# Rests of the gated values made three blocks early in the v pass of a PEER layer

## The chip, the cores and the metric

The kernel runs on one core of a Trainium2 chip. The metric is the device time of one execution in microseconds; the time given is the median of the runs. The profile is one execution of the same program, read with the hardware profiler.

## The reference, cut to what matters

The program is a chain of four transformer layers over 256 tokens of width 1024, in float32. The first two end in a PEER layer: 8 heads choose 16 each of 16384 experts per token, and the output is a sum over the chosen experts' rows of `v`, weighted by the gelu of the hidden values times the gate.

```python
def block(args):
    xb, eb, gb = args
    h = jnp.einsum('td,thkd->thk', xb, u[eb], preferred_element_type=jnp.float32)
    a = (jax.nn.gelu(h, approximate=False) * gb).astype(xb.dtype)
    return jnp.einsum('thk,thkd->td', a, v[eb])
```

Only the last line, for each of the two PEER layers, is touched by the change.

## The kernel before, in words

The kernel does not gather experts. It computes the hidden value of every one of the 16384 experts for all 256 tokens (the u pass), multiplies it by a gate that is zero for an expert that was not chosen, and multiplies the resulting 256 x 16384 matrix by all of `v` (the v pass). Both passes go in 128 blocks of 128 experts. A block of `u` or `v` is 128 x 1024 float32, 512 KB.

TensorE works on float32r values, and a float32 product is made of three matmuls (`mm3`, line 354): each operand is split into a rounded value and its rest (value minus rounded value), and rounded x rounded, rounded x rest and rest x rounded are added up. So each operand costs one rounding on ScalarE and one subtraction on VectorE.

The v pass, block n (of `peer_pe`, lines 1328 to 1341): for two halves of the tokens and two halves of the width one `mm3` each, 12 matmuls of 512 columns. They read

- `Ar[n % 4]`: the gated values of block n, 128 x 256, rounded (`gated_act`, line 1343, on ScalarE) and their rest (`gated_dve`, line 1352, on VectorE), four buffers;
- `whi[n']`: the block of `v`, rounded (`round_block`, line 1199, on ScalarE), three buffers, taken in turn;
- `ring_rest`: the rest of that block (`rest_block`, line 1207, on VectorE). It lies over `ring`: the rest is written in place of the raw block, in one of seven slots, which SyncE's queue fills from memory (`load`, line 275) as soon as the block seven before has been used.

The names: `("y", l, n)` is signalled by TensorE (semaphore `psum_complete`) when block n of the v pass of layer l is done. `round_block` of v block k waits for `y` of block k - 3, which frees its `whi` buffer; `gated_act` of block n waits for `y` of block n - 4. Every rest, that of a gated block and that of a v block alike, counts one semaphore up, `weights_rest` (`lo`), in VectorE's order; every rounding counts up `weights_rounded` (`hi`). TensorE waits at the head of block n for `lo.at(("Ar", l, n))` and `lo.at(("v", l, n))`.

Each engine has one instruction stream, written out by hand, and takes it in order. In the v pass they are:

```python
for n in range(125):                          # ScalarE, lines 1382 to 1384
    round_block(act, l, 128 + n + 3)
    gated_act(act, l, n + 3)
for n in range(128):                          # VectorE, lines 1417 to 1420
    gated_dve(dve, l, n)
    if n < 126:
        rest_block(dve, l, 130 + n)
```

(`round_block(act, l, 128 + k)` is v block k.) So after `y` of block k ScalarE rounds v block k + 3 and then gated block k + 3; VectorE makes the rest of v block k + 3, and behind it the rest of gated block k + 2. GpSimd does nothing in the v pass.

The functions that the diff touches, with the line numbers of the profile:

Of the kernel before, what the change touches and what calls it, by code (L numbers as in the profile page):

```python
# [195 lines left out]
def build(nc, io, out, consts, where):  # L196
    ctx = ExitStack()
    with ctx:
# [90 lines left out]
        def raw(name):  # L289
            return ring[:, slot[name], :]  # L290
# [72 lines left out]
        def step(e, ins):  # L363

            sig = vec if e.name == "V" else acted if e.name == "A" else gps
            ins.then_inc(*sig.next())
            e.wait_ge(*sig.now())
# [92 lines left out]
        def project_all(e, projs, xk, ahead=0, hooks=None):  # L460

            names = [(pr["name"], g) for pr in projs for g in range(2)]
            for i in range(-1, len(names)):
                if ahead <= i + 1 < len(names):
                    if e.name == "S":
                        load_unit(e, names[i + 1])
                    elif e.name == "A":
                        round_unit(e, names[i + 1])
                    elif e.name == "V":
                        rest_unit(e, names[i + 1])  # L470
                if i < 0:
                    continue
                if e.name == "P":
                    project_pe(e, i // 2, projs[i // 2], i % 2, xk)
                elif e.name in "VA" and i % 2:
                    project_out(e, i // 2, projs[i // 2])
                for f in (hooks or {}).get(i, ()):
                    f(e)
# [714 lines left out]
        def block_name(l, k):  # L1193
            return ("u", l, k) if k < 128 else ("v", l, k - 128)

        def used(l, k):
            return ("h", l, k) if k < 128 else ("y", l, k - 128)

        def round_block(act, l, k):

            name = block_name(l, k)
            act.wait_ge(*ready[name])
            if k >= 3:
                act.wait_ge(*psum.at(used(l, k - 3)))
            act.activation(whi[:, k % 3, :], raw(name), ACT.Copy).then_inc(*hi.next(name))

        def rest_block(e, l, k):

            name = block_name(l, k)
            e.wait_ge(*hi.at(name))  # L1210
            ins = e.tensor_tensor(ring_rest[:, slot[name], :], raw(name), whi[:, k % 3, :].bitcast(F32), ALU.subtract)
            ins.then_inc(*(glo if k < BEFORE else lo).next(name))
# [34 lines left out]
        def gates_act(act, l, m):  # L1247

            act.wait_ge(*vec.at(("gated", l, m)))
            d = slice(DONE[m], 128)  # L1250
            act.activation(area[:, d, 8 * m:8 * m + 8], gates_at(2 * (m % 2))[:, d, :], ACT.Copy,
                           scale=1.0 / 32768.0).then_inc(*acted.next(("gates", l, m)))
# [9 lines left out]
        def hidden_act(act, l, n):  # L1262

            g, pv = GATED[n], ps[:, 6 + n % 2, 0:T]
            act.wait_ge(*psum.at(("h", l, n)))
            if g:
                if n >= 2 and GATED[n - 2]:
                    act.wait_ge(*vec.at(("h", l, n - 2)))
                ins = act.activation(hA[:, n % 2, 0:g], pv[:, 0:g], ACT.Gelu)
                if g < T:  # L1270
                    ins.then_inc(*acted.next())
            if g < T:
                ins = act.activation(area[:, n, g:T], pv[:, g:T], ACT.Gelu)
            ins.then_inc(*acted.next(("h", l, n)))
# [20 lines left out]
        def scores_out(e, l):  # L1295
            for k, (t, n0) in enumerate(SCORES):
                if "VA"[k % 2] != e.name:
                    continue
                e.wait_ge(*psum.at(("scores", l, t, n0)))
                o, i = Sc[:, t, n0:n0 + 4, :], bank(k).rearrange("p (n k) -> p n k", n=4)  # L1300
                if e.name == "V":
                    e.tensor_copy(o, i).then_inc(*vec.next(("scores", l, t, n0)))
                else:
                    e.activation(o, i, ACT.Copy).then_inc(*acted.next(("scores", l, t, n0)))
# [38 lines left out]
        def gated_act(act, l, n):  # L1343

            act.wait_ge(*vec.at(("gated", l, 31)))
            if GATED[n]:
                act.wait_ge(*vec.at(("h", l, n)))
            if n >= 4:
                act.wait_ge(*psum.at(("y", l, n - 4)))
            act.activation(Ar[:, n % 4, 0, :], area[:, n, :], ACT.Copy).then_inc(*hi.next(("Ar", l, n)))  # L1350

        def gated_dve(dve, l, n):
            dve.wait_ge(*hi.at(("Ar", l, n)))
            dve.tensor_tensor(Ar[:, n % 4, 1, :], area[:, n, :], Ar[:, n % 4, 0, :].bitcast(F32), ALU.subtract).then_inc(
                *lo.next(("Ar", l, n)))

        def peer_act(act, l, xk):
            project_all(act, projP[l], xk, 2)
            scores_out(act, l)
            for k in range(3):  # L1360
                round_block(act, l, k)
            wide_at = {16: ("dA", 0), 17: ("dA", 1), 18: ("tB", 0), 19: ("tB", 1)}
            for kind, n in EVENTS:
                if kind == "h":
                    round_block(act, l, n + 3)
                    hidden_act(act, l, n)
                    if n in wide_at:
                        what, t = wide_at[n]
                        d = tb[t]
                        o, i = (d["dAr"], d["dA"]) if what == "dA" else (d["tBr"], d["tf"][:, :, 1, :])  # L1370
                        act.wait_ge(*vec.at(("dA", l, t)))
                        act.activation(o, i.unsqueeze(3).to_broadcast(H16), ACT.Copy).then_inc(*acted.next(("wide", l, t, what)))
                    if n == 32:
                        for t in both:
                            act.wait_ge(*vec.at(("ex", l, t)))
                            act.activation(tb[t]["res"][:, 2, :, :], tb[t]["res"][:, 2, :, :], ACT.Exp).then_inc(
                                *acted.next(("ex", l, t)))
                elif kind == "gate":
                    gates_act(act, l, n)
            for n in range(3):  # L1380
                gated_act(act, l, n)
            for n in range(125):
                round_block(act, l, 128 + n + 3)
                gated_act(act, l, n + 3)

        def peer_pool(pool, l, xk):
            for n in range(BEFORE):
# [2 lines left out]
        def peer_dve(dve, l, xk):  # L1390
            project_all(dve, projP[l], xk, 2)
            scores_out(dve, l)
            topk_dve(dve, l)
            for t in both:
                dve.wait_ge(*psum.at(("res", l, t)))
                dve.tensor_copy(jT[:, :, t * 128:(t + 1) * 128], ps[:, 4 + t, 0:256].rearrange("p (r k) -> p r k", r=2)).then_inc(
                    *vec.next())
                dve.tensor_scalar(gr[:, t * 128:(t + 1) * 128], ps[:, 4 + t, 256:384], 32768.0, None, ALU.mult).then_inc(
                    *vec.next(("gr", l, t)))
            dve.wait_ge(*vec.now())  # L1400
            step(dve, dve.tensor_copy(gk[:, 0, :], gr))
            step(dve, dve.tensor_tensor(gr, gr, gk[:, 0, :], ALU.subtract))
            dve.tensor_copy(gk[:, 1, :], gr).then_inc(*vec.next(("gk", l)))
            one_hots_dve(dve, l, 0)
            for k in range(BEFORE, BEFORE + 2):
                rest_block(dve, l, k)
            for kind, n in EVENTS:
                if kind == "gate":
                    gates_dve(dve, l, n)
                elif kind == "h" and n >= BEFORE:  # L1410
                    rest_block(dve, l, n + 2)
                    if GATED[n - 1]:
                        hidden_dve(dve, l, n - 1)
                    if n % 2 == BEFORE % 2 and 1 <= GATED[n] // 8 < 32:
                        one_hots_dve(dve, l, GATED[n] // 8)
            hidden_dve(dve, l, 127)
            for n in range(128):
                gated_dve(dve, l, n)
                if n < 126:
                    rest_block(dve, l, 130 + n)  # L1420

        def topk_dve(dve, l):

# [141 lines left out]
        for h in range(6):  # L1565
            for t in range(2):
                n = 128 * (t + 1)
# [264 lines left out]
        for h in range(8):  # L1832
            kv = h // 4
            o = 64 * kv
            for t in range(2):
# [14 lines left out]
                n = 128 * (t + 1)  # L1850
# [4 lines left out]
        for h in range(8):  # L1855
            o = 64 * (h % 2)
            for t in range(2):
                n = 128 * (t + 1)
# [584 lines left out]
```

## Time and profile before

| | |
|---|---|
| median of 3 runs | 3196.44 us (3195.13 to 3197.36) |
| profiled execution, its own time | 3195.85 us |
| span of the profiled execution | 3194.0 us |
| TensorE matmuls busy, share of the span | 2989.4 us, 94% |
| VectorE busy | 1987.9 us, 62% |
| ScalarE busy | 1328.6 us, 42% |
| GpSimd busy | 371.0 us, 12% |
| mean granted TensorE clock | 0.935 of full speed |
| moved from and to memory | 478.74 MB, mean 150 GB/s |

The span runs from the first to the last instruction; some 2 us of the execution's own time lie around it. The v pass of the first PEER layer lies at 683 to 1056 us of the span, that of the second at 1723 to 2098 us. "PE" is TensorE's matmuls, "PEld" its weight loads, which run beside the matmuls; "DVE" is VectorE, "ACT" ScalarE, "POOL" GpSimd, "SP" SyncE, whose queue issues the transfers.

### The profile page before, as it was taken

The page shows a single profiled execution, that of the slowest core. Times are in us where ns is not written, and L with a number is a line of the kernel's source. Part 1 is how long each engine was busy: PE and PEld are TensorE (multiplying, and loading weights), DVE is VectorE, ACT ScalarE, POOL GpSimd, SP SyncE. Part 2 cuts the span into 40 slices and gives each one's busy share as a digit, 9 for nine tenths or more (in the row PEclk, how much of TensorE's full clock was granted, in tenths as well). Part 3 has the DMA queues.
Part 4 walks back from the last instruction along what each step waited for, and adds up shares of the span by engine and source line. Part 5 has one row for each costly group of instructions (what it writes and reads, how often), then busy time and mean ns, then how long its engine had stood idle before and what let it go on. Part 6 is the DMA issues. An engine that isn't in the chain of part 4 may idle for free.

```text
span 3194.0 us, 46441 instructions
## 1 busy us (share of the span) xinstructions
PE 2989.4 (94%) x19008; PEld 2639.5 (83%) x19008; DVE 1987.9 (62%) x3739; ACT 1328.6 (42%) x2130; POOL 371.0 (12%) x205
## 2 busy tenths in 40 slices
PE   8879999999999798999999999979989998989997
PEld 7779999987777787999998777767668997878997
DVE  4668978955555556796895555564665545455555
ACT  3333544444444343454444444432333433433332
POOL 0015910000000111591000000021000001010000
PEclk9889999999999998999999999987579999879999
DMA  5244544455555534454445445543025554324553
GB/s 189 90 140 139 177 148 159 153 178 180 182 178 181 159 129 133 140 178 147 158 159 171 179 181 181 178 129 119 1 87 162 175 179 160 115 54 159 177 180 112
DMA packets 223316, 478.74 MB, mean 150 GB/s; under 512 B 27120, under 2 KB 108032, under 8 KB 223104
## 3 DMA queue, kind: packets, MB, share of 16 engines
q1 hardware_dynamic: 220144, 473.29, 45.6%
q8 instruction: 150, 2.46, 0.3%
q10 hardware_dynamic: 2960, 2.49, 0.2%
q14 instruction: 62, 0.51, 0.1%
HBM read 474.14 MB, written 1.57 MB: 149 GB/s over the span
## 4 chain that ended last, share of the span: by engine, by line
PE 78%; DVE 12%; ACT 6%; POOL 2%; issue 1%; DMA 0%; ACTq 0%; DVEq 0%; SPq 0%; POOLq 0%
PE ps L133 76%; DVE ring_rest L148 4%; ACT whi L139 4%; PE ps L136 2%; POOL ring_rest L148 2%; DVE big L156 1%; DVE Ar L148 1%; DVE st L152 1%; ACT big L139 1%; DVE spl L148 1%; DVE xb L156 1%; DVE big L148 1%; DVE st L156 0%; DVE st L172 0%; DVE xr L148 0%
## 5 line engine op out<-in xcount | busy, mean ns | idle before, releaser
L139 ACT ACTIVATE whi<-ring 128x1024 fp32r<-128x1024 f32 x512 | 542.7, 1061 | 747.1 <-PE ps L133 747.0
L133 PE MATMUL ps<-xr,whi 128*128 128x256 f32 x4096 | 753.4, 286 | 11.0 <-POOL ring_rest L148 10.5
L148 DVE TENSOR_TENSOR ring_rest<-ring,whi 128x1024 fp32r<-128x1024 f32 x412 | 503.6, 1223 | 383.9 <-ACT whi L139 383.9
L133 PE MATMUL ps<-whi,Ar 128*128 128x512 f32 x2048 | 671.3, 399 | 12.6 <-DVE Ar L148 4.5
L133 PE MATMUL ps<-xr,spl 128*128 128x256 f32 (+1 forms) x5256 | 653.0, 287 | 7.9 <-DVE xr L148 4.0
L133 PEld LDWEIGHTS ps<-xr,spl 128*128 128x128 f32 (+1 forms) x5256 | 647.7, 194 | 14.2 <-issue 5.4
L133 PEld LDWEIGHTS ps<-xr,whi 128*128 128x128 f32 x4096 | 643.2, 193 | 13.8 <-DVE big L178 8.6
L148 DVE TENSOR_TENSOR spl<-ring,spl 128x1024 fp32r<-128x1024 f32 (+4 forms) x356 | 401.9, 1170 | 378.3 <-ACT spl L139 378.1
L133 PE MATMUL ps<-xr,ring_rest 128*128 128x256 f32 x2048 | 581.9, 284 | 0.0
L133 PEld LDWEIGHTS ps<-whi,Ar 128*128 128x128 f32 x2048 | 384.9, 188 | 158.5 <-DVE Ar L148 72.1
L139 ACT ACTIVATE spl<-ring 128x1024 fp32r<-128x1024 f32 (+3 forms) x384 | 366.3, 1002 | 273.7 <-PE ps L133 265.9
L133 PE MATMUL ps<-ring_rest,Ar 128*128 128x512 f32 x1024 | 401.4, 392 | 0.0
L133 PEld LDWEIGHTS ps<-xr,ring_rest 128*128 128x128 f32 x2048 | 395.8, 193 | 0.0
L139 ACT ACTIVATE big<-ps 128x256 f32<-128x256 f32 (+25 forms) x415 | 152.7, 368 | 352.1 <-PE ps L133 188.5
L148 POOL TENSOR_TENSOR ring_rest<-ring,whi 128x1024 fp32r<-128x1024 f32 x100 | 267.3, 2691 | 163.2 <-ACT whi L139 162.6
L148 POOL TENSOR_TENSOR spl<-ring,spl 128x1024 fp32r<-128x1024 f32 (+1 forms) x28 | 57.3, 2069 | 1894.7 <-ACT spl L139 1894.7
L133 PE MATMUL ps<-spl,xr 128*128 128x512 f32 (+2 forms) x1152 | 245.6, 374 | 6.9 <-DVE spl L148 3.8
L133 PEld LDWEIGHTS ps<-spl,xr 128*128 128x128 f32 x1152 | 204.6, 196 | 44.6 <-DVE spl L148 4.6
L133 PEld LDWEIGHTS ps<-ring_rest,Ar 128*128 128x128 f32 x1024 | 192.9, 188 | 32.3
L133 PE MATMUL ps<-big 128*128 128x64 f32 (+9 forms) x752 | 207.6, 423 | 4.6 <-DVE big L148 1.8
L133 PEld LDWEIGHTS ps<-big 128*128 128x128 f32 (+3 forms) x752 | 156.1, 270 | 61.4 <-issue 38.4
L133 PE MATMUL ps<-spl,Ar 128*128 128x512 f32 x768 | 183.6, 395 | 0.0
(107 smaller groups left out, 2202.0 us busy)
## 6 DMA issues: line engine op xcount, KB each, us to landing
ring<-in_peer_u_dram SPq DMA_DIRECT2D x256, 512.0 KB, 3.5
ring<-in_peer_v_dram SPq DMA_DIRECT2D x256, 512.0 KB, 3.4
ring<-in_moe_w_gate_dram SPq DMA_DIRECT2D x64, 512.0 KB, 4.1
ring<-in_moe_w_up_dram SPq DMA_DIRECT2D x64, 512.0 KB, 4.2
ring<-in_moe_w_down_dram SPq DMA_DIRECT2D x64, 512.0 KB, 4.1
ring<-in_peer_w_q_dram SPq DMA_DIRECT2D x32, 512.0 KB, 4.2
ring<-in_sb_w_in_dram SPq DMA_DIRECT2D x24, 512.0 KB, 4.3
ring<-in_ab_w_in_dram SPq DMA_DIRECT2D x20, 512.0 KB, 4.8
```

What stands on the lines that cost most here:

```text
L133: return self.e.matmul(o, l, r, start=start, stop=stop)
L136: return self.e.transpose(o, i, ident)
L139: return self.e.activation(o, i, f, **k)
L148: return self.e.tensor_tensor(o, a, b, op)
L152: return self.e.tensor_scalar(o, a, s1, None, op0)
L156: return self.e.scalar_tensor_tensor(out=o, in0=a, scalar=s, in1=b, op0=op0, op1=op1)
```

## The change

VectorE makes the rests of gated blocks 0, 1 and 2 ahead of its loop, and in the loop that of block n + 3 behind the rest of v block n + 2. ScalarE rounds gated block n + 3 ahead of v block n + 3 instead of behind it. Nothing is added or taken away: both kernels have the same instructions, apart from waits.

```diff
@@ ScalarE, peer_act
             for n in range(3):
                 gated_act(act, l, n)
             for n in range(125):
+                gated_act(act, l, n + 3)
                 round_block(act, l, 128 + n + 3)
-                gated_act(act, l, n + 3)
@@ VectorE, peer_dve
             hidden_dve(dve, l, 127)
-            for n in range(128):
+            for n in range(3):
                 gated_dve(dve, l, n)
-                if n < 126:
-                    rest_block(dve, l, 130 + n)
+            for n in range(126):
+                rest_block(dve, l, 130 + n)
+                if n + 3 < 128:
+                    gated_dve(dve, l, n + 3)
```

VectorE's stream where the v pass of the first layer begins, with the semaphores that an instruction waits for. `Ar<-big,Ar` is the rest of a gated block, `ring_rest<-ring,whi` that of a v block; `big<-hA,big` belongs to the u pass. Before (gated 0, v 2, gated 1, v 3, gated 2, v 4):

```order
L148 TENSOR_TENSOR big<-hA,big 128x256 [waits scalar_result] x2
L148 TENSOR_TENSOR Ar<-big,Ar 128x256 [waits weights_rounded]
L148 TENSOR_TENSOR ring_rest<-ring,whi 128x1024
L148 TENSOR_TENSOR Ar<-big,Ar 128x256 [waits weights_rounded]
L148 TENSOR_TENSOR ring_rest<-ring,whi 128x1024 [waits weights_rounded]
L148 TENSOR_TENSOR Ar<-big,Ar 128x256
L148 TENSOR_TENSOR ring_rest<-ring,whi 128x1024 [waits weights_rounded]
```

With the change (gated 0, 1, 2, then v 2, gated 3, v 3, gated 4, v 4):

```order
L148 TENSOR_TENSOR big<-hA,big 128x256 [waits scalar_result] x2
L148 TENSOR_TENSOR Ar<-big,Ar 128x256 [waits weights_rounded] x3
L148 TENSOR_TENSOR ring_rest<-ring,whi 128x1024
L148 TENSOR_TENSOR Ar<-big,Ar 128x256 [waits weights_rounded]
L148 TENSOR_TENSOR ring_rest<-ring,whi 128x1024 [waits weights_rounded]
L148 TENSOR_TENSOR Ar<-big,Ar 128x256 [waits weights_rounded]
L148 TENSOR_TENSOR ring_rest<-ring,whi 128x1024 [waits weights_rounded]
```

The two kinds still alternate, but each gated rest in the loop belongs to a block two later than before, and it now carries a wait for ScalarE of its own.

ScalarE's stream at the same place, `Ar<-big` being a rounded gated block and `whi<-ring` a rounded v block (v 3, v 4 and v 5 here). Before:

```order
L139 ACTIVATE hA<-ps 128x256 [waits vector_result]
L139 ACTIVATE Ar<-big 128x256 x3
L139 ACTIVATE whi<-ring 128x1024 [waits psum_complete,ring6_landed]
L139 ACTIVATE Ar<-big 128x256
L139 ACTIVATE whi<-ring 128x1024 [waits psum_complete,ring0_landed]
```

With the change:

```order
L139 ACTIVATE hA<-ps 128x256 [waits vector_result]
L139 ACTIVATE Ar<-big 128x256 x4
L139 ACTIVATE whi<-ring 128x1024 [waits psum_complete,ring6_landed]
L139 ACTIVATE Ar<-big 128x256
L139 ACTIVATE whi<-ring 128x1024 [waits psum_complete,ring0_landed]
```

Gated block 3 comes ahead of the first wait for TensorE, and from there on a rounded v block is followed by gated block k + 4 instead of k + 3 (k being the block whose end ScalarE waited for).

## Rows read from the trace of the kernel before

**Rows 1.** Page, part 4: the chain that ended last, shares of the span by engine
```profile
PE 78%; DVE 12%; ACT 6%; POOL 2%; issue 1%; DMA 0%; ACTq 0%; DVEq 0%; SPq 0%; POOLq 0%
```
**Rows 2.** Windows: us, busy (x instructions) by engine, clock, DMA share, GB/s
```profile
450.00:650.00 200.00, 199.74 (x1883) 198.02 (x1882) 173.64 (x257) 95.61 (x202) 0.00 (x0) 1.00 0.49 158
690.00:1048.00 358.00, 354.36 (x1473) 268.14 (x1472) 191.80 (x246) 166.76 (x246) 0.00 (x0) 1.00 0.54 181
1732.00:2088.00 356.00, 351.81 (x1466) 267.19 (x1465) 190.39 (x244) 166.50 (x245) 0.00 (x0) 1.00 0.52 180
```
**Rows 3.** Waits, 682 to 1058 us: waiter, releaser, us in total, times, longest
```profile
ACT whi L139 <- PE ps L133: 195.6, 125, 3.0
DVE ring_rest L148 <- ACT whi L139: 171.2, 125, 2.8
PEld ps L133 <- DVE Ar L148: 36.3, 84, 2.5
```
**Rows 4.** Chain that ended last, 896 to 902 us: start, us, what
```profile
896.01 3.04 PE ps L133 x12
...
899.13 1.07 ACT whi L139
...
900.23 1.23 DVE ring_rest L148
901.45 0.35 DVE Ar L148
...
901.84 3.04 PE ps L133 x12
```
**Rows 5.** Timeline, weight loads at four block heads [idle before <-releaser]
```profile
688.76 0.19 PEld L133 LDWEIGHTS ps<-whi,Ar 128*128 128x128 f32 x1 [0.51 <-DVE Ar L148]
...
1047.87 0.19 PEld L133 LDWEIGHTS ps<-whi,Ar 128*128 128x128 f32 x1 [0.46 <-DVE Ar L148]
...
1730.60 0.19 PEld L133 LDWEIGHTS ps<-whi,Ar 128*128 128x128 f32 x1 [0.49 <-DVE Ar L148]
...
2089.66 0.19 PEld L133 LDWEIGHTS ps<-whi,Ar 128*128 128x128 f32 x1 [0.51 <-DVE Ar L148]
```
**Rows 6.** Timeline, matmuls between two stalls, first and last: start, us
```profile
902.18 0.39 PE L133 MATMUL ps<-ring_rest,Ar 128*128 128x512 f32 x1
...
907.19 0.39 PE L133 MATMUL ps<-whi,Ar 128*128 128x512 f32 x1
```
**Rows 7.** Timeline, matmuls of the last blocks, first and last
```profile
1048.20 0.39 PE L133 MATMUL ps<-ring_rest,Ar 128*128 128x512 f32 x1
...
1055.99 0.39 PE L133 MATMUL ps<-whi,Ar 128*128 128x512 f32 x1
```
**Rows 8.** Timeline of VectorE, the rest of v block 2
```profile
682.81 1.22 DVE L148 TENSOR_TENSOR ring_rest<-ring,whi 128x1024 fp32r<-128x1024 f32 x1
```
**Rows 9.** Tile Ar: durations ns min/median/max, first and last start
```profile
L139 ACT ACTIVATE Ar<-big x256: 397/400/407, 682.0 to 2090.6; 128x256 fp32r<-128x256 f32 x128
L148 DVE TENSOR_TENSOR Ar<-big,Ar x256: 415/418/421, 682.5 to 2092.2; 128x256 fp32r<-128x256 f32 x128
```
**Rows 10.** Tile in_peer_v_dram: issues of v blocks, and time to landing
```profile
DMA to landing us min/median/max: 3.2/3.4/4.9
```
**Rows 11.** Waits of SyncE's queue, 690 to 1060 us
```profile
SPq L193 <- PE ps L133: 324.1, 126, 2.8
```
**Rows 12.** Windows across the head of the second v pass
```profile
1716.00:1724.00 8.00, 5.73 (x44) 5.43 (x43) 4.75 (x7) 4.17 (x9) 0.00 (x0) 0.95 0.57 195
1724.00:1727.00 3.00, 3.00 (x9) 2.37 (x9) 0.60 (x2) 0.00 (x0) 0.00 (x0) 0.56 0.01 5
```
**Rows 13.** Timeline, the slow matmuls at that head
```profile
1724.21 1.06 PE L133 MATMUL ps<-whi,Ar 128*128 128x512 f32 x2
1725.06 0.63 PE L133 MATMUL ps<-ring_rest,Ar 128*128 128x512 f32 x1
```

## The prediction

> **What bounds the kernel now.** I read the chain of waits first, because it says which engine has to become shorter. Three quarters of it are TensorE's [rows 1]; DVE has 12% and ACT 6%, so there are places where TensorE waits for those two. Next I put windows over the stages, since the change touches two stages only. The second thing to see is in [rows 2]: in the u pass (450 to 650 us) TensorE has no gap, 199.74 of 200 us. In the two v passes it is short by 3.6 and 4.2 us of 358 and 356, which looks like nothing. But the end of a matmul is modelled, and the 0.39 us row of a matmul whose successor comes 0.23 us later covers a part of any gap behind it. So busy time can't size a short stall; only distances between starts can. The waits show that the stall is there: the weight loads waited 84 times for the rest of a gated block in the first v pass, 36.3 us in all [rows 3]. One of these, 2.5 us, is the head of the pass. The others average (36.3 - 2.5) / 83 = 0.41 us.
>
> The chain through the middle of a v pass tells why [rows 4]. It is a closed loop. Twelve matmuls of block k (3.04 us with the drain of the last), then ACT rounds v block k + 3 (1.07), DVE makes its rest (1.23), DVE makes the rest of gated block k + 2 (0.35 beyond its overlap with the instruction ahead), and then block k + 2 may start. From one head to the other it is 901.84 - 896.01 = 5.83 us, for two blocks. What TensorE waits for is the last of these, a 128x256 subtraction of 0.42 us [rows 9] whose inputs have been there for most of a block: its rounding, done after `y` of block k - 1, is over before this loop begins. It is late only because it stands behind the rest of v block k + 3, which nobody needs until the block after. That is a matter of order, and order is what the change alters.
>
> **What a block costs without the stall.** I need the distance of two matmuls where nothing waits. Between two stalls, from the second matmul of one head to the last but none before the next, 22 distances take 907.19 - 902.18 = 5.01 us, 0.2277 us each [rows 6]. That stretch has one full turn of ACT and DVE work in it and most of a second. In the last blocks of the pass, 34 distances take 1055.99 - 1048.20 = 7.79 us, 0.2291 us each [rows 7]. I take the middle, 0.2284; a block of 12 is then 2.741 us (2.732 to 2.749). The stalled pace comes from the heads of blocks 2 and 125 [rows 5]: (1047.87 - 688.76) / 123 = 2.920 us a block in the first pass, (2089.66 - 1730.60) / 123 = 2.919 in the second.
>
> At one place a page would give another figure. The rows say 0.228 us per matmul of 512 columns at a granted clock of 1.00 [rows 2, 6]. The Trainium skill, page "TensorE: Matmul & The Clock Gate", section "Back-to-back issue gap", has a fixed 2.5 ns above columns / 2.4 for isolated gaps, 216 ns at 512 columns; by it a free block would be 2.59 us, and the gain nearly double. The measured stretches, in which no wait is recorded, do not agree, so the sum goes by them.
>
> **The change part by part.** *VectorE.* In the loop the gated rest behind v block n + 2 becomes that of block n + 3 instead of n + 1. Its input is ready in time: ACT rounds gated block n + 3 right behind v block n + 2, 0.40 us [rows 9], and is done at some 1.07 + 0.40 = 1.5 us after `y` of block n - 1, while DVE is busy with the v rest until 1.07 + 1.23 = 2.3 us after it [rows 4]. So the new wait for ACT before each gated rest costs nothing, and nothing but the next v rest is queued behind it. The gated rest is then done 2.7 us after `y` of block n - 1 and used three blocks, 8.2 us, after it, so it leaves TensorE's path. That takes out the whole stall: 2.920 - 2.741 = 0.179 us a block, times 123 blocks, 22.0 us in each v pass and 44 us in both. *What is late next.* A block's head now waits for the rest of its own v block: 3.04 + 1.07 + 1.23 us and some 0.1 us of hand-overs after the head of a block three earlier, 5.4 us, against 3 x 2.741 = 8.2 us that TensorE needs to get there. There are 2.8 us of slack. The second loop, over the gated values, is y, rounding of v, rounding and rest of the gated block, 5.8 us at most over four blocks, 11.0 us. Neither engine is full: ACT has 1.5 us and DVE 1.6 us of work in a block of 2.74 us.
>
> *Head of the pass.* DVE makes two gated rests more before the rest of v block 2: 2 x 0.35 us. That rest would be done at 682.81 + 0.7 + 1.2 = 684.7 us [rows 8], and block 2 starts at 688.76 - 0.51 = 688.2 us at the earliest [rows 5]: 0. The first block waits for gated rest 0, which is where it was: 0. *ACT.* The exchange puts gated block 3 ahead of the first wait for TensorE; afterwards both roundings follow the same `y` in the same order as before: 0 by itself. It is what gives DVE its input early enough. *End of the pass.* The last three blocks are free already [rows 7]: 0.
>
> *Transfers.* 512 KB a block at 2.741 us is 191 GB/s instead of 181. The queue waits for freed slots, not for the memory, in 324 of 370 us [rows 11], a transfer lands 3.4 us after its issue, 4.9 at worst [rows 10], and has four blocks, 11 us, until its rounding. A window of 8 us shows 195 GB/s [rows 12]. So 0; if the cover were gone, the pace would be the memory's, which is a rival below.
>
> **Sum.** Two passes give 44.0 us (46 by 0.2277, 42 by 0.2291). Against the profiled execution's own 3195.85 us (span 3194.0) this is 3151.9 us. The median of the runs is 0.6 us above that execution, so 3152.5 us, 1.4% less.
>
> One term has no row: the clock. Where TensorE comes back from a pause it sometimes runs at the lower level for some matmuls; at the head of the second v pass the granted clock is 0.56 for 3 us [rows 12] and matmuls stand 0.427 us apart [rows 13], 8 of them, 1.6 us. Work behind the first v pass moves ahead by 22 us, behind the second by 44, and such places may gain or lose one of these by chance. I allow 5 us to either side and take 0.
>
> **The rivals.** *Memory limits the pace (3%).* If transfers could do no more than some 187 GB/s in a long stretch, a block would take 524.3 / 187 = 2.80 us, the gain would be 0.12 x 246 = 29 us: 3167 us. Against it: every wait of ACT in front of a v rounding was ended by TensorE, none by a transfer [rows 3].
>
> *No effect (4%).* Memory holds it at 181 GB/s, or the wait at the head hides another that comes at the same moment, since both rests count one semaphore: 3196 us. For it speaks only that the profile can't tell which count was missing. Against it, the head follows the end of the gated rest by 0.04 us in the chain, and in the old order that rest is the later count.
>
> *Slower (2%): the clock falls.* The stalls go and 128 blocks follow each other without a pause. If the chip answered with its lower level, each matmul would cost 0.427 instead of 0.228 us. From 44 / 0.199 = 221 matmuls of 3072 on, the kernel is slower; with a tenth of them, 307, it is at 3213 us. Against it: the u pass holds a clock of 1.00 with TensorE busy without a gap for 200 us [rows 2].
>
> *The free matmul is faster than I measured (1%).* If matmuls were held up by a hidden wait throughout, and took 0.216 us once that is gone, a block would take 2.592 us and the gain be 0.328 x 246 = 81 us: 3116 us. That is the rule of the page named above. Against it stand the stretches in which nothing waits.
>
> **How the numbers follow.** The forecast has 90%. A difference from no change can be told from 0.2% on, 6.4 us. Faster by more: the forecast, the memory rival at 187 GB/s and the fast matmul, 94%. Within: 4%. Slower: 2%. The range takes the forecast with its bounds for the matmul, 42 to 46 us, and 5 us for the clock, 3145 to 3160 us, and a few us more toward the memory's case: 3144 to 3164 us.
>
> **What would show it.** Right: in the profile after, the waits of the weight loads for DVE's gated rest vanish but for the head of each pass (from 84 to one or two); the chain in a v pass is TensorE's alone; heads of blocks 2 and 125 are 337 us apart, not 359; windows in it show 191 GB/s; ACT's roundings of `v` begin every 2.74 us. Wrong: a wait of ACT for a transfer, a wait of TensorE at block heads for the v rest, or a clock under 1.00 inside a v pass. The u passes and all else must keep their length.

## The result and the profile after

| | before | after |
|---|---|---|
| median | 3196.2 us (4 runs, 3195.13 to 3197.36) | 3144.91 us (4 runs, 3143.21 to 3145.74) |
| profiled execution | 3195.85 us | 3143.21 us |
| span | 3194.0 us | 3141.4 us |
| mean granted clock | 0.935 | 0.935 |

The ratio of the runs is 0.9839, with a 95% interval of 0.9825 to 0.9852: 51.3 us less, 1.6%. The forecast was 3152.5 us, with a range of 3144 to 3164 us.

The chain that ended last, by engine (the page's part 4 of the changed kernel), against [rows 1]:

```profile
PE 87%; DVE 7%; ACT 2%; POOL 2%; issue 1%; DMA 0%; DVEq 0%; SPq 0%; ACTq 0%; POOLq 0%
```

DVE and ACT have lost nine points of the chain, though their busy times haven't changed by a microsecond. TensorE's busy time has fallen from 2989.4 to 2945.1 us, for the same 19008 matmuls: 44 us of its busy time before were waiting and slower matmuls. Windows inside the two v passes, with the columns of [rows 2]:

```profile
690.00:1022.00 332.00, 332.00 (x1467) 274.90 (x1466) 190.53 (x245) 166.53 (x244) 0.00 (x0) 1.00 0.58 193
1710.00:2040.00 330.00, 330.00 (x1457) 273.27 (x1456) 188.53 (x241) 164.86 (x241) 0.00 (x0) 1.00 0.57 193
```

TensorE's busy time has no gap left in either. The clock stays at 1.00, and the memory moves 193 GB/s instead of 181. The waits of the changed kernel in the first pass, 682 to 1036 us, against [rows 3]:

```profile
ACT whi L139 <- PE ps L133: 170.8, 125, 2.7
DVE ring_rest L148 <- ACT whi L139: 145.8, 125, 2.1
```

The wait of the weight loads for DVE's gated rest, 36.3 us before, isn't among them. What is left of it is the head of each pass, 2.5 us; in the first pass it ends at 681.61 us, just ahead of this window, and in the second (1690 to 2056 us) it is the only one, against 79 before:

```profile
PEld ps L133 <- DVE Ar L148: 2.5, 1, 2.5
```

ACT and DVE still wait; they wait for TensorE, as engines with time to spare should. ACT's stream (timeline, 869 us and on) is even:

```profile
869.69 1.06 ACT L139 ACTIVATE whi<-ring 128x1024 fp32r<-128x1024 f32 x1 [1.35 <-PE ps L133]
870.65 0.40 ACT L139 ACTIVATE Ar<-big 128x256 fp32r<-128x256 f32 x1
872.41 1.06 ACT L139 ACTIVATE whi<-ring 128x1024 fp32r<-128x1024 f32 x1 [1.35 <-PE ps L133]
```

A block is 872.41 - 869.69 = 2.72 us, against 2.92 before and 2.741 forecast; the heads of blocks 2 and 125 stand 334.6 us apart, where 337 had been forecast. Last, the first and last matmul of the first v pass (timeline of TensorE), and of the second:

```profile
681.61 0.50 PE L133 MATMUL ps<-whi,Ar 128*128 128x512 f32 x1 [2.27 <-DVE Ar L148]
...
1029.68 0.39 PE L133 MATMUL ps<-whi,Ar 128*128 128x512 f32 x1
...
1694.44 0.80 PE L133 MATMUL ps<-whi,Ar 128*128 128x512 f32 x1 [2.27 <-DVE Ar L148]
...
2044.10 0.39 PE L133 MATMUL ps<-whi,Ar 128*128 128x512 f32 x1
```

The passes take 348.1 and 349.7 us. Before, the first and last matmuls stood at 682.94 and 1055.99 us, and at 1723.19 and 2097.78: 373.1 and 374.6 us. So the v passes gave 25.0 + 24.9 = 49.9 us of the 52.6 us between the two profiled executions. The other 2.7 us came about outside of them, where both programs are the same: 1.3 us ahead of the first pass, 2.4 us between the passes, and 1.0 us lost again behind the second. Single executions of one kernel differ as much, so this isn't shown to be a gain of the change.

### The profile page after: what moved, and what is told of

Its sections match the earlier page's. It is cut to its first block, busy times and chain, and to the rows that moved or that the text cites. A ratio compares the mean times of both kernels' runs of the same rounds, so it can differ in the third digit from the quotient of the medians.

```text
span 3141.4 us, 46693 instructions
## 1 busy us (share of the span) xinstructions
PE 2945.1 (94%) x19008; PEld 2652.7 (84%) x19008; DVE 1987.8 (63%) x3739; ACT 1327.9 (42%) x2130; POOL 371.6 (12%) x205
## 4 chain that ended last, share of the span: by engine, by line
PE 87%; DVE 7%; ACT 2%; POOL 2%; issue 1%; DMA 0%; DVEq 0%; SPq 0%; ACTq 0%; POOLq 0%
PE ps L133 86%; PE ps L136 2%; POOL ring_rest L148 2%; DVE big L156 1%; DVE st L152 1%; ACT big L139 1%; DVE spl L148 1%; DVE xb L156 1%; DVE big L148 1%; ACT whi L139 0%; DVE st L156 0%; DVE xr L148 0%; DVE st L172 0%; POOL big L148 0%; ACT L139 0%
## 5 line engine op out<-in xcount | busy, mean ns | idle before, releaser
L133 PE MATMUL ps<-whi,Ar 128*128 128x512 f32 x2048 | 632.1, 390 | 4.5 <-DVE Ar L148 4.5
```

The source lines that it names most:

```text
L133: return self.e.matmul(o, l, r, start=start, stop=stop)
```

## The experiments

All edits are against one of the two kernels, in the two functions that the change touches unless said otherwise. The times of before beside them are medians of 3195.39 us (9 runs; for the experiments on the moved wait and on the head of the pass) and 3195.27 us (13 runs; for the other four).

### VectorE's order alone

```diff
             hidden_dve(dve, l, 127)
-            for n in range(128):
+            for n in range(3):
                 gated_dve(dve, l, n)
-                if n < 126:
-                    rest_block(dve, l, 130 + n)
+            for n in range(126):
+                rest_block(dve, l, 130 + n)
+                if n + 3 < 128:
+                    gated_dve(dve, l, n + 3)
```

> VectorE's new order with ScalarE's old one. My theory (the stall is the gated rest standing behind the rest of a v block that is needed a block later): the order on VectorE is all of it. Gated block n + 3 is now rounded after y of block n, so its rest is done 1.9 us after it and is needed 5.4 us after it; no stall comes back. 3145 us, weight loads wait for the gated rest twice only. Rival (the two edits are needed together, since VectorE's v rests now queue behind a gated rest that comes a block later): part of the stall returns as a wait for the v rest, 3160 to 3196 us.

Measured: 3144.84 us (3143.03 to 3148.01), ratio 0.984 (0.9823 to 0.9856). All of the gain is there without ScalarE's swap. DVE's timeline in this kernel:

```profile
869.56 0.43 DVE L148 TENSOR_TENSOR Ar<-big,Ar 128x256 fp32r<-128x256 f32 x1 [1.16 <-ACT Ar L139]
869.90 1.22 DVE L148 TENSOR_TENSOR ring_rest<-ring,whi 128x1024 fp32r<-128x1024 f32 x1
872.28 0.43 DVE L148 TENSOR_TENSOR Ar<-big,Ar 128x256 fp32r<-128x256 f32 x1 [1.16 <-ACT Ar L139]
```

DVE now idles in front of the gated rest and makes the v rest behind it. The v rest starts 1.74 us after its own rounding began (at 868.16 us), against 1.09 us in the changed kernel, so it is 0.65 us later. It still ends 2.2 us before the head of its block, instead of 2.9, so TensorE doesn't see it. In its own waits (682 to 1036 us) the weight loads appear once:

```profile
DVE Ar L148 <- ACT Ar L139: 146.5, 125, 2.8
...
PEld ps L133 <- DVE Ar L148: 2.5, 1, 2.5
```

The rival that needed both edits is out.

### ScalarE's order alone

```diff
             for n in range(125):
+                gated_act(act, l, n + 3)
                 round_block(act, l, 128 + n + 3)
-                gated_act(act, l, n + 3)
```

> ScalarE's new order with VectorE's old one. My theory: the loop y, rounding of v, rest of v, gated rest, head is untouched, 5.83 us for two blocks, so 3196 us as before and the same 80 waits a pass. Rival (ScalarE's order matters by itself): under 3185 us.

Measured: 3196.76 us (10 runs, 3194.18 to 3200.03), ratio 1.0007 (0.9998 to 1.0017). No difference. The waits in the first pass, 682 to 1058 us, are those of before within a few per cent (the weight loads wait 37.6 us in all, against 36.3):

```profile
ACT whi L139 <- PE ps L133: 195.3, 125, 2.7
DVE ring_rest L148 <- ACT whi L139: 171.1, 125, 2.8
PEld ps L133 <- DVE Ar L148: 37.6, 93, 2.5
```

Half of the edit is idle. The prediction priced ScalarE's exchange at 0 "by itself" and added that it gives DVE its input early enough. The addition was wrong: DVE's input comes early enough in the old order too, as the run before this one shows.

### One block early instead of two

```diff
-            for n in range(128):
+            for n in range(2):
                 gated_dve(dve, l, n)
-                if n < 126:
-                    rest_block(dve, l, 130 + n)
+            for n in range(126):
+                rest_block(dve, l, 130 + n)
+                gated_dve(dve, l, n + 2)
```

> ScalarE's order as before; VectorE makes the gated rest of block n + 2 behind the rest of v block n + 2, one block earlier than the kernel before and one later than the change. My theory: what counts is only that the last instruction of the loop isn't one that the next head needs, so one block is as good as two: 3145 us. Rival (the gain grows with the lead): about 3170 us, half of the gain.

Measured: 3144.76 us (3143.36 to 3148.88), ratio 0.9844 (0.9827 to 0.986). One block of lead is worth as much as two. Between these two kernels the gain is a threshold, not a slope: once the head of the next block doesn't need the last instruction of the loop, moving it further bought nothing.

### The wait moved instead of the work

VectorE and ScalarE as in the kernel before; TensorE waits later (in `peer_pe`, with `mm3` written out):

```diff
-                pe.wait_ge(*lo.at(("Ar", l, n)))
+                pe.wait_ge(*hi.at(("Ar", l, n)))
                 pe.wait_ge(*lo.at(("v", l, n)))
...
+                        pe.matmul(o, a[0], w[0], n == 0, False)
+                        pe.matmul(o, a[0], w[1], False, False)
+                        if t == 0 and d == 0:
+                            pe.wait_ge(*lo.at(("Ar", l, n)))
+                        ins = pe.matmul(o, a[1], w[0], False, n == 127)
```

> The kernel before in both orders; TensorE waits for the rest of the gated block not at the head of the v block but ahead of its third matmul, the first that reads it (at the head it waits for the rounded gated block instead). My theory (a closed loop of 5.83 us for two blocks): the loop becomes shorter by two matmuls, 0.46 us, to 5.37 us, under the 5.44 us that TensorE itself needs, so the stall goes with no order changed: 3145 to 3150 us. Rival (a wait inside a group of matmuls holds up the weight loads and costs something at each block, 0.1 us x 256): 3170 us. Rival 2 (the true wait was for the rest of v): 3196 us.

Measured: 3147.06 us (3144.44 to 3148.77), ratio 0.985 (0.9835 to 0.9865). The sum over the loop holds: 5.83 us less two matmuls is under what TensorE needs for two blocks, and the stall is gone with every instruction of ACT and DVE in its old place. It also settles that the missing count was the gated rest, not the rest of `v`, since the wait for the rest of `v` stayed at the head. It is 2.4 us above the changed kernel, which lies near the spread of the runs, but its v passes are 350.0 and 351.5 us, 1.9 us longer each. Matmuls from one block into the next (timeline of TensorE):

```profile
907.62 0.39 PE L133 MATMUL ps<-ring_rest,Ar 128*128 128x512 f32 x1
...
908.30 0.40 PE L133 MATMUL ps<-ring_rest,Ar 128*128 128x512 f32 x1
...
909.00 0.39 PE L133 MATMUL ps<-ring_rest,Ar 128*128 128x512 f32 x1
...
909.70 0.39 PE L133 MATMUL ps<-ring_rest,Ar 128*128 128x512 f32 x1
...
910.38 0.39 PE L133 MATMUL ps<-ring_rest,Ar 128*128 128x512 f32 x1
```

Three distances take 0.68, then 0.70, 0.70 and 0.68 us: the matmuls are slower for a while without any recorded wait. It happens in every second block, which takes 2.74 or 2.75 us; the blocks between take 2.720 us. That leads to the next run.

### Thirty stalls put back

The changed kernel, with the gated rest of every eighth block where it was:

```diff
             for n in range(126):
                 rest_block(dve, l, 130 + n)
-                if n + 3 < 128:
+                if (n + 1) % 8 == 0:
+                    gated_dve(dve, l, n + 1)
+                if n + 3 < 128 and (n + 3) % 8:
                     gated_dve(dve, l, n + 3)
```

> The changed kernel, but the gated rest of every eighth block (8, 16, ... 120) is made where the kernel before makes it, 15 stalls in a pass and 30 in all. It asks why a free matmul takes 0.2267 us after the change where 0.2277 to 0.2291 was read before it. Theory A (a stall also slows the matmuls that follow it, for a block or so, until the weight loads are ahead again): in the block behind a stall the matmuls stand 0.233 us apart, elsewhere 0.2267; a stall costs 0.24 us at the head and 0.05 to 0.15 us behind it, 3154 to 3157 us. Theory B (something else slowed them in that execution, such as ScalarE and VectorE beside them at another phase, or the chip): 0.2267 everywhere or evenly more, and 30 x 0.24 = 7 us, 3152 us.

Measured: 3161.7 us (3161.07 to 3162.36), ratio 0.9894 (0.9878 to 0.9911): above both ranges. The waits show the stalls, 15 and the head of the pass (682 to 1040 us):

```profile
PEld ps L133 <- DVE Ar L148: 10.4, 16, 2.5
```

The timeline of TensorE across one of them:

```profile
704.58 0.98 PE L133 MATMUL ps<-whi,Ar 128*128 128x512 f32 x2
705.40 0.40 PE L133 MATMUL ps<-ring_rest,Ar 128*128 128x512 f32 x1
...
706.10 0.40 PE L133 MATMUL ps<-ring_rest,Ar 128*128 128x512 f32 x1
...
706.79 0.40 PE L133 MATMUL ps<-ring_rest,Ar 128*128 128x512 f32 x1
...
707.49 0.39 PE L133 MATMUL ps<-ring_rest,Ar 128*128 128x512 f32 x1
...
708.18 0.39 PE L133 MATMUL ps<-ring_rest,Ar 128*128 128x512 f32 x1
708.40 0.61 PE L133 MATMUL ps<-whi,Ar 128*128 128x512 f32 x2
...
711.58 0.39 PE L133 MATMUL ps<-ring_rest,Ar 128*128 128x512 f32 x1
```

From 704.58 to 705.40 are two distances, 0.82 instead of 0.45 us: the stall itself, 0.37 us with the second distance, that of the first matmul after the wait. Then three distances take 0.70, 0.69, 0.70, 0.69 us, 0.232 us each. Further on, from 708.18 to 711.58, 15 distances take 3.40 us: 0.2267 us each, which is the changed kernel's figure. ACT and DVE work beside both. So theory A holds in kind: the slow matmuls come behind a stall and end within a block. The neighbours' work by itself isn't their cause: with VectorE's order alone the v rest runs 0.65 us later against the matmuls than in the changed kernel, and a block takes 2.720 us in both. Over the 15 blocks of the first pass, the mean distances behind the head are 0.233, 0.232 and 0.233 us and fall to 0.227 us by the tenth. A stall costs 0.40 us in all (0.38 to 0.42 in 14 of the 15, 0.65 in one).

In size, the expectation was short twice. First, of the 0.40 us only 0.03 lie in the slow matmuls; 0.37 us are the two distances at the head, where 0.24 had been expected. The passes here take 354.2 and 355.6 us, 6.1 and 6.0 more than in the changed kernel: 12.1 us for 30 stalls, where 9 to 12 had been expected. Second, the other 5 us between the medians aren't in the v passes at all. Between the two profiled executions there are 18.6 us: 12.1 in the v passes, 4.6 between them, 1.3 ahead of the first and 0.7 behind the second. Here are the windows over the same 1561 matmuls behind the first v pass, first of the changed kernel, then of this one:

```profile
1029.70:1289.00 259.30, 218.29 (x1561) 202.69 (x1560) 150.33 (x353) 99.43 (x162) 42.22 (x36) 0.93 0.40 132
```

```profile
1037.10:1301.00 263.90, 222.81 (x1561) 207.07 (x1560) 151.06 (x358) 99.51 (x162) 42.25 (x36) 0.91 0.40 130
```

The same work takes 4.6 us more, 4.5 of them TensorE's busy time, at a mean granted clock of 0.91 instead of 0.93. This stage is full of short pauses of TensorE, and the program comes to it 7 us later here. In the seven experiments and the changed kernel the stretch from the end of the first v pass to the head of the second took 663 to 669 us, for the same instructions. But the moment of arrival alone doesn't pick the value. The kernel with VectorE's order alone and the changed kernel in its second set of runs (the control of the last experiment) both ended the first v pass at 1030.9 us, and took 668.4 and 665.0 us for the stretch. Their windows over it, in this order, with the same 5094 matmuls:

```profile
1030.90:1699.00 668.10, 618.92 (x5094) 600.35 (x5092) 490.99 (x1033) 296.86 (x519) 168.06 (x82) 0.96 0.48 151
```

```profile
1030.90:1695.60 664.70, 615.66 (x5094) 596.87 (x5092) 495.77 (x1033) 297.13 (x519) 166.18 (x82) 0.97 0.48 152
```

So single executions differ here by 3.4 us at the same arrival. All four runs of the kernel with thirty stalls agree within 1.3 us, which speaks for something of its own that holds it at the long end; what that is stays open.

### The head of the pass

The changed kernel, with gated blocks 0 to 2 made ahead of the last hidden block of the u pass:

```diff
@@ ScalarE
             for kind, n in EVENTS:
                 if kind == "h":
+                    if n == 127:
+                        for k in range(3):
+                            gated_act(act, l, k)
                     round_block(act, l, n + 3)
...
-            for n in range(3):
-                gated_act(act, l, n)
@@ VectorE
-            hidden_dve(dve, l, 127)
             for n in range(3):
                 gated_dve(dve, l, n)
+            hidden_dve(dve, l, 127)
```

> The changed kernel, with gated blocks 0, 1 and 2 rounded ahead of the last hidden block of the u pass, and their rests made ahead of VectorE's last product of the u pass. Only the head of each v pass is concerned, where TensorE waits 2.27 us for the first gated rest. My theory: these waits go, 2.3 us in each pass, and the lower clock behind the pause with them where it came (1.6 us): 3139 to 3141 us. Rival (something else is as late at that point, such as the rest of the first v block or the banks): 3145 us.

> The changed kernel once more, beside the one before it on the same chip, to tell a gain of 5 us from the spread of a chip: 3145 us by every theory.

Measured on one chip, five runs each: 3139.47 us (3137.21 to 3140.32) for this one and 3144.63 us (3143.17 to 3145.78) for the changed kernel; the two sets don't overlap. The first weight load of the v pass in this kernel:

```profile
679.34 0.19 PEld L133 LDWEIGHTS ps<-whi,Ar 128*128 128x128 f32 x1 [0.47 <-DVE Ar L148]
```

It waits 0.47 us, against 2.48 in the changed kernel; twice 2.0 us is 4.0 of the 5.2 us. The clock at the second head gives 1.6 us more: that v pass now takes 348.1 us and not 349.7. Together they are 5.6 us, 0.4 more than was measured, and the stretches that no edit touches differ by more than that between executions. Windows there, of the changed kernel (0.52 behind its pause of 2.27 us), and of this one:

```profile
1695.00:1698.00 3.00, 3.00 (x9) 2.34 (x8) 1.53 (x3) 0.00 (x0) 0.00 (x0) 0.52 0.02 7
```

```profile
1680.00:1702.00 22.00, 21.73 (x143) 19.84 (x143) 12.70 (x21) 11.78 (x20) 0.00 (x0) 1.00 0.57 179
```

This is the fastest kernel of the study, ratio 0.9824 (0.981 to 0.9837) to the kernel before.

## Why the prediction was right, and where it was off

**The mechanism.** "It is late only because it stands behind the rest of v block k + 3" is shown by five runs: VectorE's order alone brings all of the gain, ScalarE's alone none, one block of lead suffices, the same stall goes when the wait is put two matmuls later, and it comes back at 15 heads of a pass when 15 gated rests are put back. The closed loop read from the chain, 5.83 us for two blocks against what TensorE needs by itself, was the right object to add up.

**What is late next.** Nothing, as forecast: in the changed kernel a v rest ends 2.9 us before the head of its block (2.8 had been forecast), and even the order that delays each v rest by 0.65 us took nothing from TensorE.

**The term that was mis-sized: the free matmul.** The prediction took 0.2284 us, between 0.2277 and 0.2291 read in two stretches "where nothing waits" [rows 6, 7]. It is 0.2267 us: a block is 2.720 us and not 2.741, which over 246 blocks is 0.021 x 246 = 5.2 us. Both stretches began right behind a stall, where the matmuls are slow for most of a block, and both contain a second block whose weights came late. In the first, two weight loads at the next head last 0.51 us together instead of 0.41, with no wait recorded. In the second, the head of block 126 has a recorded wait of 0.18 us, so it isn't true that nothing waits there, nor that the last three blocks were free already. The timelines of the weight loads of before, in this order:

```profile
904.25 0.51 PEld L133 LDWEIGHTS ps<-whi,Ar 128*128 128x128 f32 x2
...
1050.64 0.19 PEld L133 LDWEIGHTS ps<-whi,Ar 128*128 128x128 f32 x1 [0.18 <-DVE Ar L148]
```

With the right pace, two blocks lose 2 x (2.920 - 2.720) = 0.40 us to a stall, and not the 2 x 0.179 = 0.36 us of the sum. The bounds, 42 to 46 us, were made from these two stretches and so both lay on one side; the measured gain of the passes is 49.9 us. The 7.6 us from the forecast to the measured median are these 5.2 us, 0.7 in the blocks that weren't counted, 1.4 outside the v passes, and 0.2 by which the median of before is lower with its fourth run. What brought the time into the range was the allowance for the clock, not the bound of the matmul, and that was luck: 3144.91 us lies 0.9 us above the range's lower end, and just under the 3145 us that the bounds and the allowance give.

**The blocks counted.** 123 of 128 blocks were priced. Behind the slow matmuls at its head, all distances in a pass are 0.2267 us now, and blocks outside the 123 gave the 0.7 us that is left: 44.0 + 5.2 + 0.7 = 49.9. Read from the starts directly, they gave 0.24 us in the first two blocks and 0.19 us in the last three of each pass, 0.9 us in all; the difference is rounding.

**The clock.** 5 us to either side, taken as 0, was a fair size: between the two profiled executions the identical stretches outside the v passes differ by 2.7 us, and over all kernels the stretch between the passes differs by up to 6 us. Between the medians, 51.3 us, it leaves 1.4 us.

**The rivals.** "No effect" fell with the result, and the moved wait settles what it left open: the missing count was the gated rest. Memory as the limit fell at once: 193 GB/s held in both passes. The clock didn't fall in a v pass without a pause. A free matmul of 0.216 us didn't come; the 0.2267 us lie 0.011 us above the figure for isolated gaps of the Trainium skill's page "TensorE: Matmul & The Clock Gate", section "Back-to-back issue gap", with TensorE waiting for nothing.

## What to carry to other kernels

When a chain of waits closes on itself, divide its length by the blocks it advances and compare it with the bound engine's own time. Then look for an instruction at its end that stands behind work needed later, and put it one place earlier. More lead than that bought nothing here. And when the pace without a stall has to be read from a trace full of stalls, take it from as far behind a stall as there is room: busy time hides the gap, and the matmuls right behind it are still slow.

## What was not expected of the hardware

After a wait at the head of a block, TensorE's matmuls of 512 float32r columns stood 0.233 us apart, falling to 0.2267 us by about the tenth, at a granted clock of 1.00 and with no wait recorded; a wait before the third matmul that shows no idle time did the same in every second block (0.70 us for three instead of 0.68). The kernel before shows it too at the heads between two stalls, 61 in each pass, where the first matmul comes in step (0.229 us behind the last one): their blocks take 2.75 us on average in the first pass and 2.74 in the second, instead of 2.720. Why isn't known. ACT's and DVE's work by itself isn't the cause, since blocks take 2.720 us beside the same work in the kernels without late weights, and nothing more was tried.
